# Expert loops of a two-layer decoder: the order of the weight loads in two of seven steps, and the bank and place of a quarter of the token gather

## What is computed

```python
h = (jax.nn.silu(jnp.einsum('td,edf->tef', xt, w_gate))
     * jnp.einsum('td,edf->tef', xt, w_up))
h = h * comb[:, :, None].astype(h.dtype)      # comb: two experts per token, inside one group of four
return jnp.einsum('tef,efd->td', h, w_down)
```

## Time and profile before

| | us |
|---|---|
| median of 3 runs | 767.24 (767.23 to 768.08) |
| the profiled execution, whole | 766.43 |
| its span | 764.4 |
| PE busy | 738.0 (97%) |
| PE idle, put down to loads of downs | 9.4 |
| granted clock of PE, mean | 0.995 |

### The profile page before, as it was taken

One profiled execution on the slowest core, in us unless ns is written; L12 is line 12 of the kernel. 1 busy time (PEld: TensorE's weight loads), 2 busy tenths in 40 slices (PEclk: granted clock), 3 DMA queues, 4 the chain that ended last, 5 costly groups with the idle time before them and its releaser, 6 DMA issues.

```text
span 764.4 us, 10586 instructions
## 1 busy us (share of the span) xinstructions
PE 738.0 (97%) x4068; PEld 437.0 (57%) x4069; DVE 292.2 (38%) x521; ACT 240.9 (32%) x455; POOL 109.5 (14%) x68
## 2 busy tenths in 40 slices
PE   9999999999999899999999999999999899999994
PEld 6989887644353353353799878644353353335332
DVE  5689927642111110120667656742111111112114
ACT  5556356332111111120735666332111111112112
POOL 2133000067000000002140000067000000000013
PEclk9999999999999999999999999999999999999998
DMA  8998335959999999999995435959999999994311
GB/s 319 304 389 321 113 110 220 385 219 423 418 424 421 423 421 400 423 421 415 388 388 204 135 142 220 382 236 422 422 422 422 421 423 408 424 421 157 166 55 55
DMA packets 51446, 246.13 MB, mean 322 GB/s; under 512 B 6265, under 2 KB 6482, under 8 KB 26834
## 3 DMA queue, kind: packets, MB, share of 16 engines
q1 hardware_dynamic: 51410, 245.65, 80.9%
HBM read 244.58 MB, written 1.05 MB: 321 GB/s over the span
## 4 chain that ended last, share of the span: by engine, by line
PE 74%; DMA 15%; DVE 6%; ACT 2%; issue 2%; POOL 0%; SPq 0%; POOLq 0%; ACTq 0%; DVEq 0%
PE ps L1936 20%; DMA ring<-in_moe_w_down 12%; PE ps L1948 12%; PE ps L1737 11%; PE ps L1732 10%; PE ps L1922 3%; DMA ring<-in_moe_w_up 3%; PE ps L1903 3%; PE ps L1693 2%; DVE ring_lo L1117 2%; PE ps L1987 2%; PE ps L1665 1%; PE ps L1911 1%; PE ps L2019 1%; PE ps L1773 1%
## 5 line engine op out<-in xcount | busy, mean ns | idle before, releaser
L1936 PE MATMUL ps<-ring,scratch 128*64 128x512 f32 x576 | 140.4, 593 | 0.4 <-DMA ring<-in_moe_w_up 0.4
L1948 PE MATMUL ps<-ring,scratch 128*64 128x512 f32 x512 | 114.3, 596 | 9.4 <-DMA ring<-in_moe_w_down 9.4
L1117 DVE TENSOR_TENSOR ring_lo<-ring,w_hi 128x2048 fp32r<-128x2048 f32 x36 | 83.4, 2332 | 18.4 <-ACT w_hi L741 18.1
L1936 PEld LDWEIGHTS ps<-ring,scratch 128*64 128x64 f32 x576 | 47.1, 137 | 71.1 <-issue 69.3
L698 POOL TENSOR_TENSOR scratch<-rounded,gate 128x256 f32<-128x256 f32 x16 | 14.1, 882 | 493.5 <-PE ps L2080 310.0
L1948 PEld LDWEIGHTS ps<-ring,scratch 128*64 128x64 f32 x512 | 36.6, 137 | 75.6 <-issue 73.1
L741 ACT ACTIVATE w_hi<-ring 128x2048 fp32r<-128x2048 f32 x35 | 66.7, 1914 | 28.6 <-PE ps L1737 15.7
L1533 DVE TENSOR_TENSOR scratch<-ps,scratch 128x512 f32<-128x512 f32 x16 | 11.1, 692 | 157.4 <-PE ps L1936 157.4
L1544 DVE SCALAR_TENSOR_TENSOR rounded<-ps,gslot,rounded 128x512 fp32r<-128x512 f32 x32 | 24.0, 751 | 107.1 <-ACT rounded L988 107.1
L1936 PE MATMUL ps<-spare,scratch 128*64 128x512 f32 x256 | 56.3, 592 | 0.0
L1936 PE MATMUL ps<-scratch 128*64 128x512 f32 x192 | 56.2, 592 | 0.0
(11 more groups left out here) (297 smaller groups left out, 1089.9 us busy)
## 6 DMA issues: line engine op xcount, KB each, us to landing
ring<-in_moe_w_down SPq DMA_DIRECT2D x64, 1024.0 KB, 13.3
ring<-in_moe_w_up SPq DMA_DIRECT2D x40, 1024.0 KB, 14.8
ring<-in_moe_w_gate SPq DMA_DIRECT2D x32, 1024.0 KB, 10.8
spare<-in_moe_w_gate SPq DMA_DIRECT2D x32, 1024.0 KB, 14.9
scratch<-in_moe_w_up SPq DMA_DIRECT2D x24, 1024.0 KB, 19.6
ring<-in_a_w_in SPq DMA_DIRECT2D x15, 1024.0 KB, 12.9
ring<-in_kv_w SPq DMA_DIRECT2D x8, 1024.0 KB, 15.1
ring<-in_a_w_out SPq DMA_DIRECT2D x4, 1024.0 KB, 14.6
```

The source lines that it names most:

```text
L1117: V.tensor_tensor(ring_lo[:, piece_slot(i), :, :], ring[:, piece_slot(i), :, :], w_hi[:, i % HI, :, :].bitcast(F32), ALU.subtract).then_in ...
L1936: last = mm(ps[half, bank, :], xe[:, HALF_K * part + k, own], weight(odd, matrix, part, e)[:, k, :], start=part == 0 and k == 0, stop=part ...
L1948: last = mm(ps[half, bank, :], hT[:, 2 * part + k, half], weight(odd, DOWN, part, e)[:, 2 * k + cols, :], start=part == 0 and k == 0, stop ...
```

## The change

There are two edits, and the amount of work is the same.

**The order of the loads.** The lists are cut in four (next gates, next ups, last up, downs), and steps 3 and 4 are written in another order. Steps 1, 2, 5, 6 and 7 issue the same sequence as before.

**The gather.** In even pairs the third quarter (`k` 4 and 5) is written to bank B and not to bank A, and the second half of the gather stands before the transposes of `pick_g`, which go to bank A and not to B. PE's wait for `ht_ready` (ACT has copied `hid` out of bank A) moves behind the gather. ACT and DVE take `xe` before `gslot` and `put`. Since the transposes of an even pair are in bank A, which the next pair's gates use, PE's wait for `put_done` moves from the ups to the gates, in all pairs.

```diff
+            NEXT_GATES = ((GATE, 0, BOTH), (GATE, 1, BOTH))
+            NEXT_UPS = ((UP, 0, BOTH), (UP, 1, (0,)))
+            LAST_UP = ((UP, 1, (1,)),)
+            DOWNS = ((DOWN, 0, BOTH), (DOWN, 1, BOTH))
...
                     elif p < 5:
-                        order = REST[0:1] + FIRST + REST[1:]
+                        order = LAST_UP + NEXT_GATES + DOWNS + NEXT_UPS
...
+                    pe.wait_ge(put_done, c0 + i + 1)
                     into_hidden(BANK_A, two, odd, GATE, gate_ps)
...
-                    pe.wait_ge(put_done, c0 + i + 1)
                     into_hidden(BANK_B, two, odd, UP, up_ps)
...
+                    if not odd:
+
+                        gather(range(4, 6), (BANK_B,))
+                        pe.wait_ge(xe_dve, gathered(layer, two, 0) + 1)
+                        gather(range(6, 8), (BANK_D,)).then_inc(xe_ps, 1)
+                        pe.wait_ge(ht_ready, pair + 1)
...
-                    pe.wait_ge(ht_ready, pair + 1)
-                    if not odd:
+                    if odd:
+                        pe.wait_ge(ht_ready, pair + 1)
+                    else:
                         pe.wait_ge(xe_act, gathered(layer, two, 0) + 1)
-                        pe.wait_ge(xe_dve, gathered(layer, two, 0) + 1)
-                        gather(range(4, 8), (BANK_A, BANK_D))
```

More of the change, by code:

```diff
@@ L552, in _ @@
             BOTH = (0, 1)
-            FIRST = ((GATE, 0, BOTH), (GATE, 1, BOTH), (UP, 0, BOTH), (UP, 1, (0,)))
-            REST = ((UP, 1, (1,)), (DOWN, 0, BOTH), (DOWN, 1, BOTH))
+            NEXT_GATES = ((GATE, 0, BOTH), (GATE, 1, BOTH))
+            NEXT_UPS = ((UP, 0, BOTH), (UP, 1, (0,)))
+            LAST_UP = ((UP, 1, (1,)),)
+            DOWNS = ((DOWN, 0, BOTH), (DOWN, 1, BOTH))
             for layer in range(LAYERS):
@@ L582, in _ @@
                     if p < 3:
-                        order = FIRST + REST
+                        order = NEXT_GATES + NEXT_UPS + LAST_UP + DOWNS
                     elif p < 5:
-                        order = REST[0:1] + FIRST + REST[1:]
-                    else:
-                        order = REST + FIRST
-                    load_step(layer, p, p % 2, order if p < PAIRS - 1 else REST)
+                        order = LAST_UP + NEXT_GATES + DOWNS + NEXT_UPS
+                    elif p < PAIRS - 1:
+                        order = LAST_UP + DOWNS + NEXT_GATES + NEXT_UPS
+                    else:
+                        order = LAST_UP + DOWNS
+                    load_step(layer, p, p % 2, order)
                 def load_ln():
@@ L976, in experts @@
                                          ACT.Copy).then_inc(ht_ready, 1)
+                    if not odd:
+                        take_xe(xe_ps, gathered(layer, two, 0) + 2, BANK_B, (4, 5), slice(0, 4 * SLOTS))
                     act.wait_ge(put_ps, pair + 2)
-                    nc.scalar.activation(silu[:, 0:T], ps[:, BANK_B, 0:T], ACT.Copy, accum_out=gslot[:, 0:1]
-                                         ).then_inc(gslot_ready, 1)
-                    if not odd:
-                        take_xe(xe_ps, gathered(layer, two, 0) + 2, BANK_A, (4, 5), slice(0, 4 * SLOTS))
+                    nc.scalar.activation(silu[:, 0:T], ps[:, BANK_B if odd else BANK_A, 0:T], ACT.Copy,
+                                         accum_out=gslot[:, 0:1]).then_inc(gslot_ready, 1)
                     for part, bank, ready in ((0, BANK_C, yc_ps), (1, BANK_D, yd_ps)):
@@ L1536, in experts @@
                         take_xe(gathered(layer, two, 0) + 1, (2, 3), slice(0, 4 * SLOTS))
-                    dve.wait_ge(gslot_ready, pair + 1)
-                    V.tensor_scalar(put[:, :], ps[:, BANK_B, 0:T], 0.0, None, ALU.is_gt).then_inc(put_done, 1)
                     if not odd:
                         take_xe(gathered(layer, two, 0) + 2, (6, 7), slice(0, 4 * SLOTS))
+                    dve.wait_ge(gslot_ready, pair + 1)
+                    V.tensor_scalar(put[:, :], ps[:, BANK_B if odd else BANK_A, 0:T], 0.0, None, ALU.is_gt
+                                    ).then_inc(put_done, 1)
                     for part, bank in ((0, BANK_C), (1, BANK_D)):
@@ L1923, in gather @@
                                       pick[:, t, :, :].rearrange("p e s -> p (e s)"), start=n == 0, stop=n == 3)
-                    last.then_inc(xe_ps, 1)
+                    return last
                 def into_hidden(bank, two, odd, matrix, ends):
@@ L2062, in experts @@
                         pe.wait_ge(xr_ready, 2 * layer + 2)
-                        gather(range(0, 4), (BANK_C, BANK_D))
+                        gather(range(0, 4), (BANK_C, BANK_D)).then_inc(xe_ps, 1)
                     if odd:
@@ L2076, in experts @@
                             add_up(1)
+                    if not odd:
+                        gather(range(4, 6), (BANK_B,))
+                        pe.wait_ge(xe_dve, gathered(layer, two, 0) + 1)
+                        gather(range(6, 8), (BANK_D,)).then_inc(xe_ps, 1)
+                        pe.wait_ge(ht_ready, pair + 1)
                     pe.wait_ge(pickg_ready, pair + 1)
                     for t in range(TT):
-                        last = nc.tensor.transpose(ps[:, BANK_B, t * P:(t + 1) * P],
+                        last = nc.tensor.transpose(ps[:, BANK_B if odd else BANK_A, t * P:(t + 1) * P],
                                                    pick_g[:, t, :, :].rearrange("p e s -> p (e s)"), ident[:, :])
                     last.then_inc(put_ps, 1)
-                    pe.wait_ge(ht_ready, pair + 1)
-                    if not odd:
+                    if odd:
+                        pe.wait_ge(ht_ready, pair + 1)
+                    else:
                         pe.wait_ge(xe_act, gathered(layer, two, 0) + 1)
-                        pe.wait_ge(xe_dve, gathered(layer, two, 0) + 1)
-                        gather(range(4, 8), (BANK_A, BANK_D))
                     out_of_hidden(two, odd, 0, None if odd else gathered(layer, two, 0) + 2)
```

## The result

| | before | changed |
|---|---|---|
| median | 767.24 us (766.93 to 768.08) | 759.08 us (758.22 to 759.4) |
| profiled execution, whole | 766.43 us | 759.4 us |
| its span | 764.4 us | 757.5 us |

The ratio is 0.9896, with a 95% interval of 0.9883 to 0.9909: the change makes the kernel 1.0% faster. The forecast was 759.9 us, and the range 758.4 to 762.3.

A forecast was written before the change was run, and what follows sets the result against it. PE and the transfer queue were both taken as full. The first layer's 2.2 us and the second's 5.1 made 7.3 us off the median 767.24, so 759.9 us, range 758.4 to 762.3.

The forecast's parts named there:

- The view of two full resources: Late in the expert loop, transfer engines and PE are both full; moving one load forward moves another back.
- The hole of 0.6 us: First layer's queue, left by SP's late issue of pair 5's downs; taken as closed, so landings come 0.6 us earlier.
- Part 1: New queue order in steps 3 and 4: waits for downs of pairs 3 and 4 go, 4.96 us in the first layer.
- What is late next: End of first layer: PE waits some 2.4 us for pair 7's last up, so 2.2 us of 4.96 remain.
- Second layer: Second expert loop: 4.45 us from downs plus 0.7 from pair 0's gather, 5.1 us in all.
- That is just met: Second layer, last up of pair 6: it lands at 664.1, just when PE now wants it.
- Part 2: Moved gather: pair 0's 1.1 us wait for ACT goes; ACT's later work hides under 7.02 us of downs.
- Rival 1: The queue isn't the wall at the first layer's end; all 4.96 us arrive, 757.2 us; chance 0.05.
- rival 2: First layer gives nothing, through a queue hole or the mixer's loads giving 2.2 us back; 762.1 us; chance 0.08.
- rival 3: Order of issue doesn't set landings; four stalls stay, only pair 0 gives 0.7 us in second layer; 766.5 us; chance 0.03.
- Rival 4: PE waits for put_done at the gates of odd pairs; slower, 769.5 us if it came 1.2 us late; chance 0.04.
- The rule set against it: Transfer queue: if open loads shared the engines, an early place would buy less; sharing taken as only a chunk's tail.

The follow-up runs named there:

- Two chunks cut: Changed kernel with two first-layer chunks (gates of pair 6, part 0, both experts) cut to a sixteenth; first expert loop 202.4 us, changed kernel 206.2.

## Why the prediction was right

**The view of two full resources held.** The landings came to 0.1 us: the last down of pair 3 was put at 251.6 and came at 251.65, the last of pair 4 at 281.4 and came at 281.46, the last up of pair 7 at 351.1 (351.02), the last down of pair 7 at 361.0 (360.97). These are read off the landings of the single transfers in the trace; the chain above shows the one of 351.02. The hole of 0.6 us behind pair 4 closed.

**Part 1, the waits that go.** All eight are gone. Their size was short. I took the idle time in the rows, 4.96 us in the first layer; with the wall moved away it was worth 5.6. Most of the rest is how idle time is counted: the 16 matmuls before a wait are listed as 3.65 us, but in the changed kernel, with more matmuls right behind them, the next one starts 3.48 us after the first of them, since they overlap. A wait in the middle of such a row costs its idle time and these 0.17 us. Ahead of the first half of the downs it is 0.08. Over the four waits that makes 0.5 of the missing 0.6.

**What is late next.** The first loop was put at 2.2 us and gave 2.1. A new wait for the last up of pair 7 was put at some 2.4 us. It came in three pieces, 0.32 us at the last up of pair 6, 0.98 and 1.20 at the ups of pair 7, 2.5 us together; the 1.8 us in PE's list is the last up of pair 2, which takes in pair 0's gain, as was said. Two chunks cut show that the rest of the gain is there and hidden.

**Second layer.** 5.1 us were forecast and 4.8 came, but the terms were not right. The prediction had 4.45 from the downs and 0.7 from pair 0's gather. The run without the gather has the same second loop, so the gather gave nothing there in the end. Of its 0.7 us, 0.5 were left behind the last up of pair 2. The downs were worth 5.0, undersized as in the first layer. What failed is the sentence "That is just met": with more to gain than was reckoned, the last up of pair 6 is late after all (the chain has it landing at 641.66 + 20.38 = 662.04 and PE starting at 662.08), and it caps the sum at 4.9. With the queue's order alone PE reaches this up 0.1 us too early, so there the prediction's view that it is just met holds. That the total came near is partly luck: from the downs 0.4 us more arrived than was forecast, and of the gather's 0.7 nothing.

```profile
641.66 20.38 DMA ring<-in_moe_w_up
662.08 3.65 PE ps L1941 x16
```

**Part 2, cover.** ACT's new order hides as reckoned: in pair 0 `put` starts at 178.03, and the next gates at 183.64.

```profile
178.03 0.42 DVE L1544 TENSOR_SCALAR rounded<-ps 128x256 fp32r<-128x256 f32 x1 [0.42 <-ACT scratch L985]
```

**The rivals.** Rival 1 (all of it arrives) fell with the chain and the cut chunk, rival 2 with the equal mixers and with landings that are never over 2.6 us apart from pair 2 to the end of the first layer, rival 3 with the landings. Rival 4, the only one for slower, has no trace: no wait for `put_done` stands in PE's list.

**The rule set against it.** The Trainium skill ("DMA: Bandwidth & Descriptors", Queues, rings and completion order) says that a later transfer may finish its write before an earlier one. It left no mark here: in the changed kernel's first layer the loads landed in the order of issue, at 2.48 us each.

## What to carry to other kernels

When loads come in a queue that never runs dry, write down the landings as issue order times pace, and the times at which the consumer wants each; a removed wait counts only down to the next landing that is already late. One order change gave nothing by itself (step 3), its neighbour nearly everything (step 4), because the last late load decides. Once the consumer has caught up, look at the moment when the stream starts: a wait at the head of the queue that only one load needs costs all the loads behind it.

## What the runs showed of the hardware

I had not expected that it matters how a wait is divided. In the second layer of the kernel before, waits of 0.78 and 1.31 us with 3.65 us of matmuls between them, and 1.03 and 1.33 us one pair later, left PE's granted clock at 1.00. Brought together into one of 3.95 us, they took it to 0.50, which the rows above show from within the wait to some 5 us behind it, and this cost the second loop 1.1 us. In the first layer a wait of 3.92 us took the mean over 285 to 290 us to 0.72 but cost only 0.2 us, since the last down landed when PE was nearly through with the matmuls ahead of it. The Trainium skill ("TensorE: Matmul & The Clock Gate", What's actually happening) has activity release a throttle that is otherwise on, and the run with matmuls on zeros in the wait agrees: clock 1.00, and the 1.1 us back.

The profiled execution and the timed median differ by up to 1.2 us for one kernel, and the start of the load stream varies by as much among executions, in either layer; what is below that was read from loops and landings, not from medians.
